# Attention keys split over the two halves of the partitions, so that each score product reads 64 rows

## The reference, cut to what matters

```python
s = jnp.einsum('bqhd,bsd->bqhs', qib, k_idx)                 # indexer, 16 heads of 64
score = jnp.einsum('bqhs,bqh->bqs', jax.nn.relu(s), wb)
_, idx = lax.top_k(score, topk)                              # 256 keys of each query
...
logits = jnp.einsum('bqhd,bqkhd->bhqk', qb, k_sel) * scale   # 8 heads of 64
logits = logits - slopes * dist                              # ALiBi, masked, softmax
```

## Time and profile before

| | before |
|---|---|
| median of 3 runs | 2578.8 us (2577.88 to 2579.78) |
| the profiled execution | 2572.35 us, its span 2570.6 us |
| PE busy | 2484.9 us, 97% |
| DVE, ACT, POOL busy | 1288.5, 846.6, 1064.9 us |
| `projection` | 0 to 465 us |
| `mixers` | 466 us to about 910 us |
| `trunk` | to the end, some 1600 us |

### The profile page before, as it was taken

How to read it: one execution, slowest core, us unless ns; L and a number is a source line. 1 busy time by engine, 2 the same in 40 slices (tenths; PEclk the granted TensorE clock), 3 DMA queues, 4 the chain that set the end, 5 groups by cost and what they waited for, 6 DMA issues and landing times.

```text
span 2570.6 us, 36247 instructions
## 1 busy us (share of the span) xinstructions
PE 2484.9 (97%) x14088; PEld 2136.2 (83%) x14088; DVE 1288.5 (50%) x2467; ACT 846.6 (33%) x1394; POOL 1064.9 (41%) x622
## 2 busy tenths in 40 slices
PE   7999999889999989999999999999999999999997
PEld 7889999668888778898898888888888888888885
DVE  6799999797886433333333433323223332232224
ACT  3684222333443223222222323322333332332222
POOL 1433213454544424444344544444444444454442
PEclk9999999899999999999999999999999999999998
DMA  4101230333333234332232323332333233334331
GB/s 138 34 18 59 79 100 22 107 111 107 103 101 102 87 102 122 97 99 81 84 99 82 92 73 99 93 107 82 96 92 91 81 115 98 89 92 115 109 97 48
DMA packets 274997, 231.39 MB, mean 90 GB/s; under 512 B 10768, under 2 KB 255568, under 8 KB 274832
## 3 DMA queue, kind: packets, MB, share of 16 engines
q1 hardware_dynamic: 266640, 220.59, 28.8%
q10 hardware_dynamic: 8192, 8.52, 0.9%
HBM read 215.81 MB, written 12.71 MB: 89 GB/s over the span
## 4 chain that ended last, share of the span: by engine, by line
PE 59%; DMA 1%; POOL 1%; DVE 0%; ACT 0%; issue 0%; POOLq 0%; SPq 0%; ACTq 0%; DVEq 0%
PE banks L2013 37%; PE banks L2029 20%; PE banks L2065 1%; PE banks L2043 1%; PE banks L2052 1%; DMA cq_raw<-in_w_up 0%; PE banks L1715 0%; DMA last_draw<-in_w_down 0%; POOL dL L1931 0%; POOL wL L1920 0%; POOL wL L1924 0%; DVE y L2233 0%; ACT dH L2115 0%; DVE n_bn L1624 0%; ACT L2124 0%
## 5 line engine op out<-in xcount | busy, mean ns | idle before, releaser
L1924 POOL TENSOR_TENSOR wL<-cq_raw,wH 128x2048 fp32r<-128x2048 f32 x87 | 405.8, 4665 | 529.9 <-ACT wH L2109 529.9
L2013 PE MATMUL banks<-hL,wH 128*128 128x512 f32 (+1 forms) x1760 | 618.3, 351 | 5.0 <-ACT hid L2124 4.8
L2013 PE MATMUL banks<-hH,wL 128*128 128x512 f32 (+1 forms) x1760 | 617.3, 351 | 0.0
L2013 PE MATMUL banks<-hH,wH 128*128 128x512 f32 (+1 forms) x1760 | 615.4, 350 | 0.0
L2213 DVE TENSOR_TENSOR hid<-hid,banks 128x512 f32<-128x512 f32 (+1 forms) x110 | 64.4, 585 | 739.1 <-PE banks L2013 632.2
L2013 PEld LDWEIGHTS banks<-hL,wH 128*128 128x128 f32 x1760 | 330.6, 188 | 54.2 <-ACT hid L2124 5.9
L2013 PEld LDWEIGHTS banks<-hH,wL 128*128 128x128 f32 x1760 | 330.5, 188 | 46.4
L2013 PEld LDWEIGHTS banks<-hH,wH 128*128 128x128 f32 x1760 | 331.1, 188 | 44.9
L1931 POOL TENSOR_TENSOR dL<-last_draw,dH 128x1024 fp32r<-128x1024 f32 x88 | 220.9, 2510 | 332.0 <-ACT dH L2115 331.9
L2233 DVE TENSOR_TENSOR y<-y,banks 128x512 f32<-128x512 f32 (+1 forms) x340 | 233.1, 686 | 203.2 <-PE banks L2029 202.2
L2029 PE MATMUL banks<-dH,hidL 128*128 128x512 f32 (+1 forms) x748 | 296.4, 396 | 2.3 <-issue 2.3
(11 more groups left out here) (257 smaller groups left out, 4224.9 us busy)
## 6 DMA issues: line engine op xcount, KB each, us to landing
cq_raw<-in_w_gate SPq DMA_DIRECT2D x88, 512.0 KB, 4.7
cq_raw<-in_w_up SPq DMA_DIRECT2D x88, 512.0 KB, 5.9
last_draw<-in_w_down SPq DMA_DIRECT2D x88, 512.0 KB, 3.4
w_out_part<-in_w_out SPq DMA_DIRECT2D x60, 512.0 KB, 4.0
va<-in_w_in SPq DMA_DIRECT2D x10, 1024.0 KB, 5.4
va<-in_x SPq DMA_DIRECT2D x8, 512.0 KB, 4.3
vg_scratch<-y ACTq DMA_DIRECT2D x32, 128.0 KB, 1.7
y<-in_x SPq DMA_DIRECT2D x8, 512.0 KB, 7.4
```

Of the source, the lines that this page charges most:

```text
L1924: nc.gpsimd.tensor_tensor(wL[:, ff % 2, :, :, :].rearrange("p g k f -> p (g k f)"), raw[:, :, :, :].rearrange("p g k f -> p (g k f)"), wH[ ...
L2013: last = nc.tensor.matmul(banks[:, GU + (2 * q + g) % 3, 0:n], wt[:, ff % 2, g, k, :], h[:, k, a:a + n], start=(k == 0 and part == 0), sto ...
```

## The change

Keys 0 to 511 of every head now lie in partitions 0 to 63, keys 512 to 1039 in partitions 64 to 127 (`kaT` becomes [128, 8 heads, 528]). The queries of a head are written to both halves, and no zeros are needed. A score product reads the 64 partitions in which its keys lie. Keys come out of PSUM in two copies of 64 partitions, one for each head of the feature tile, and the key chunks are 512, 264 and 264 columns. The scratch for the top-8 values moves into a tile that is free by then.

```diff
+KEY_SPLIT = 512
+def key_rows(a):
+    return (slice(0, HD), 0) if a < KEY_SPLIT else (slice(HD, P), KEY_SPLIT)
...
-                kaT = sb(mixer, "kaT", [P, 4, L])
+                kaT = sb(mixer, "kaT", [P, A_HEADS, L - KEY_SPLIT])
...
-    top8 = sb(c, "top8", [P, NT, 8])
+    top8 = squares[:, 0:NT * 8].rearrange("p (m e) -> p m e", m=NT)
...
-            slab_units += [(j, fm, dest, ft, a, n) for ft in range(SW // P) for a, n in CHUNKS3]
+            slab_units += [(j, fm, dest, ft, a, n) for ft in range(SW // P)
+                           for a, n in (((0, KEY_SPLIT), (KEY_SPLIT, 264), (KEY_SPLIT + 264, 264)) if dest == "ka" else CHUNKS3)]
...
             if dest == "ka":
-                nc.scalar.activation(kaT[:, half * SW // P + idx, a:a + n], banks[:, bank, 0:n], ACT.Copy)\
-                  .then_inc(slab_out, 1)
+                to, base = key_rows(a)
+                for par in range(2):
+                    last = nc.scalar.activation(kaT[to, 2 * (half * SW // P + idx) + par, a - base:a - base + n],
+                                                banks[HD * par:HD * (par + 1), bank, 0:n], ACT.Copy)
+                last.then_inc(slab_out, 1)
...
-            return nc.tensor.matmul(logits[0:n, at:at + kn], qaT[:, m % 2, h, 0:n], kaT[:, h // 2, a:a + kn],
+            r, base = key_rows(a)
+            return nc.tensor.matmul(logits[0:n, at:at + kn], qaT[r, m % 2, h, 0:n], kaT[r, h, a - base:a - base + kn],
                                     start=True, stop=True)
...
             if what == "qa":
-                if m == 0:
-                    act.wait_ge(dve_pads, 2)
-                for par in range(2):
-                    r = slice(HD * par, HD * (par + 1))
-                    to = qaT[r, m % 2, :, 0:n].rearrange("p (f two) t -> p two f t", two=2)[:, par]
-                    ins_ = nc.scalar.activation(to, four(src)[r, :, 0:n], ACT.Copy)
+                for half in range(2):
+                    for par in range(2):
+                        to = qaT[HD * half:HD * (half + 1), m % 2, :, 0:n].rearrange("p (f two) t -> p two f t", two=2)[:, par]
+                        ins_ = nc.scalar.activation(to, four(src)[HD * par:HD * (par + 1), :, 0:n], ACT.Copy)
...
         nc.vector.memset(key[:, 0, :], 0.0).then_inc(dve_pads, 1)
-        nc.vector.memset(qaT[:], 0.0).then_inc(dve_pads, 1)
```

More of the change, by code:

```diff
@@ L1510, in scores_of @@
             else:
-                dve.wait_ge(dve_pads, 3)
+                dve.wait_ge(dve_pads, 2)
             if h == 0:
```

## The result

| | before | after |
|---|---|---|
| median, us | 2575.68 | 2582.57 |
| lowest to highest, 20 runs each | 2569.08 to 2581.05 | 2574.24 to 2590.36 |
| ratio of after to before | | 1.0025 [1.0016, 1.0034] |
| the profiled execution, its span | 2572.35, 2570.6 | 2581.62, 2579.9 |
| mean granted clock of TensorE in the profiled execution | 0.990 | 0.986 |

The change costs 6.9 us, 0.25%. The forecast was -1.3 us and "no change"; the time lies in the range, on the other side of the kernel before. The two profiled executions differ by more, 9.3 us: 3.0 up to the end of `projection`, 4.1 in `mixers` and 2.1 in `trunk`, which the change doesn't touch.

The account below looks back on a forecast made before the run. VectorE bounds tile 1, TensorE tiles 5 to 7; tiles 2 to 4 are mixed. Cost 22.8, less 18.1 gain, 8.0 hidden and 0.8 in tile 8, plus 1.0 and 0.2 for copies: -1.3 us, 2577 us, range 2570 to 2585.

Parts of the forecast that it names:

- The clock: Rival: one more 13.6 us stretch at 1.2 GHz in tiles 2 to 4 costs 6.8 us, giving 2584 us; chance 0.14.
- excursions: TensorE going from 128 to 64 rows and back in a mixer step: 0.38 us each, 56 new ones, 21.3 us.
- what is hidden: Added TensorE time in the mixers that falls into later waits for VectorE and costs nothing: 8.0 us.
- the pairs' gain: Mixer tiles 4 to 8: a step's narrower score product runs beside the wider one, saving 18.1 us.
- 18.1 less 0.8: Saving from paired scores in tiles 4 to 8, less 0.8 us because tile 8 gets nearer to VectorE's own pace.
- The sum of the costs: Mixers: 22.8 us of added TensorE time, less 8.0 us hidden in waits.
- The second product waits for both halves of the first: Rival: only one half of the wide score product has company, gain 12.3 us, not 18.1; 2583 us; chance 0.12.
- Cover of 1.34: Tile 3: TensorE's 1.3 us wait for the output projection's add, with a 1.6 us wait, catches later steps' added time.
- The rival of the fuller cover: Rival: tiles 1 to 4 and 8 show none of the excursions' cost, -8.9 us, 2570 us; chance 0.20.
- ScalarE's copies: Score units before the mixers: longer key copies, 5.5 us more ScalarE work, cost +1.0 us, between nothing and 5.5.
- The queries' copies: Mixers at h = 4: two copies become four of 585 ns once a tile, +0.2 us, bounds 0 and 9.4.

Follow-up runs that it names:

- the filler: One unread 512-column product (two in tiles 1 and 2) in TensorE's h = 1 wait, tiles 1 to 6; kernel before 2570.12 us, kernel after 2571.31.
- the filled kernels: The kernel before and the kernel after, each with the filler in tiles 1 to 6: 2570.12 and 2571.31 us.
- rows64: Kernel before with scores that read the head's own 64 partitions, keys not split, nothing paired: 2592.31 us, ratio 1.0059.
- rows64_fill: Kernel before with unpaired 64-row scores, plus the filler in tiles 1 to 6: 2584.60 us, ratio 1.0040.
- fill_before: Kernel before with the filler in tiles 1 to 6, nothing else: 2570.12 us, ratio 0.9981.
- copies: Kernel before with key chunks of 512, 264, 264 and two copies of each key unit, old layout and scores: 2580.67 us, ratio 1.0023.
- the two halves: Kernel before with the key chunks of 512, 264, 264 alone, 2577.93 us; kernel before with two copies of each key unit alone, 2575.74 us.
- low128: Kernel after with tiles 0 to 3 back at 128-row scores, zeros in the upper half of the queries: 2594.79 us, ratio 1.0079.

## Why the prediction was wrong

**The step that failed** is the sum's silence on the clock. "The clock" stood among the rivals with 0.14, on the ground that more idle time in tiles 1 to 3 might give one more low stretch, 2584 us. The time came out near that rival's (2582.6), but the sum held no term for the clock, and 0.14 was low. I had seen two such stretches in the tiles, one of them right behind the wait at `gram` h = 1, and the same wait stands in tiles 1 to 6. What that ground left out is that it comes again in tiles 4 to 6, where TensorE is the bound right behind it, and that there a stretch costs its full half (6.6 us for 13.7 in tile 5). That the time fits the rival's price is partly luck, since the rival looked for its stretch in tiles 2 to 4. Over the runs mean clock fell by 0.0038: at 1.9 us per 0.001 that is 7.2 us, the whole loss. Runs with the same mean clock (0.986, 0.987, 0.988: 59 of the kernel before, 8 after) show no loss: after is 0.2, 1.9 and 2.7 us faster there. Shown besides: the stretch in tile 5 of the profile after, none in tiles 4 to 6 once the wait is filled, 11.3 us back from the filler and some 1 us left between the filled kernels. My first account of the runs, that the pairs alone do it by making the wait longer, has fallen: `rows64` has the stretch without pairs and with a wait of 0.80 us, hardly more than before. Open: by what the clock falls in one tile and holds in the next, and so what in the change makes it fall more often; 64-row scores are what the profiles point to.

**The sum itself came out near, by errors that cancel.** Tile lengths, from the first `gram` row of one tile to that of the next (tile 8 to the last output quarter), each taken from kernels in which the tile had no low stretch, in us:

| tile | before | 64 rows, no pairs | after | measured | forecast |
|---|---|---|---|---|---|
| 3 | 48.99 | 48.15 | 47.79 | -1.2 | +1.2 |
| 4 | 51.83 | 52.67 | 52.85 | +1.0 | +1.3 |
| 5 | 52.91 | 54.80 | 53.35 | +0.4 | +0.5 |
| 6 | 57.03 | 58.74 | 56.23 | -0.8 | -1.0 |
| 7 | 60.32 | 62.65 | 57.46 | -2.9 | -2.7 |
| 8 | 108.61 | 111.1 | 106.64 | -2.0 | -3.8 |

(111.1 is 112.78 less 1.7 for a short low stretch in it.) Tile 0 was +0.9 against +0.5, tile 1 nothing against +0.5, tile 2 +1.2 against +1.1. The forecast's column is its own terms by tile: 2.7 for seven excursions (3.7 in tile 8), less what is hidden, less the pairs' gain. Measured that makes -3.4 for the mixers against -2.5. The second column takes it apart. What the excursions cost, less what is hidden, is its difference from the first: from tile 3 on -0.8, +0.8, +1.9, +1.7, +2.3 and +2.5, and +0.9 in tile 2 (`rows64_fill` less `fill_before`), 9.3 us in all. The forecast had 13.8 for these tiles. The pairs' gain, the third column less the second, is 13.4 us in tiles 4 to 8, where 18.1 less 0.8 were forecast. So a cost that was some 4.5 us too high stood against a gain that was 4 us too high.

With +3.0 in `projection` in place of +1.0, the stages at full clock add up to -0.4 us, where I had -1.3; by the fit the kernel after comes out 1.2 to 2.0 us below the one before (2572.6 against 2573.8 and 2574.6). Either way the program alone is hardly changed, as forecast.

**An excursion.** 0.38 us was near but high: tile 7, which hides none, lost 2.33 us for seven, 0.33 each; tile 6, of which I had said the same, lost 1.7, 0.24 each. The sum of the costs (22.8 - 8.0 = 14.8) against 14.5 us between the filled kernels looks better than it is, since 0.0023 of mean clock, some 4 us, is in the latter.

**The pairs.** 0.67 us a step in tile 7: measured 62.65 - 57.46 = 5.2 over eight steps, 0.65. Tiles 5 and 6 gave 1.5 and 2.5 in place of 1.9 and 3.7. In tile 8 the pairs gave 4.5 where 6.9 - 0.8 were counted. VectorE's pass over the banks is late next by more than I took off, which is most of the difference: the waits of the whole tile, to be held against the 4.5 of the earlier trace rows:

```profile
PE banks L1197 <- DVE nmax L1459: 5.8, 8, 1.5
```

**"The second product waits for both halves of the first"** has fallen: the rows of two at 812.48 show the second product's first half beside the first's. Taken row by row, the trace contradicts what the Trainium skill says in "TensorE: Matmul & The Clock Gate", Part 3, that matmuls start and end strictly in program order: the second half of the wide product stands behind both first halves.

**What hides the cost** was undersized: tile 4 kept 0.8 us where I had left 1.6, and in tile 3 seven excursions made the tile shorter. Before, late in the tile (h = 5 to 7), in the kernel with the filler:

```profile
612.68 0.66 PE L1155 MATMUL banks<-ident,on 128*128 128x128 f32 x4 [1.34 <-DVE y L1539]
615.01 0.94 PE L1184 MATMUL banks<-kaT,qaT 128*128 128x400 f32 x2 [0.73 <-DVE nmax L1453]
```

The two waits, 2.07 us, are gone after (the step is 3.33 us in place of 5.40). Cover of 1.34 was counted, the wait behind it was not. Why more goes than the delay of some 0.9 us ahead of it, I leave open. The rival of the fuller cover was right for this tile alone.

**ScalarE's copies** were forecast at +1.0 between bounds 0 and 5.5, and this term was mis-sized as well: the scores take 3.0 us longer at full clock (150.97 against 148.01), and the stage ended 3.0 us later in the kernel after, whose `projection` has as much low clock as before (two stretches of 3.4 us for one of 6.8). `copies` cost 4.8 as timed, 1.2 to 2.0 by the fit. What of it is ScalarE's 6.0 us more, what TensorE's long key units beside short score units, is not settled: the two halves cost 0 and 0 alone and 4.8 together. The queries' copies (+0.2) can't be told apart except in tile 0: the tile is 0.9 us longer after but not in `rows64`, which has its 64-row products too, nor in `low128`, which has two copies there, not four.

## What to carry to other kernels

Where a change shortens TensorE's work in front of a wait for another engine, look at what that wait does to the granted clock, not only at its length: it stands in the windows' clock column, and a stretch at 1.2 GHz costs half its length wherever TensorE is the bound. Before giving such a rival a chance, count the places where the same wait comes again with TensorE as the bound behind it. To tell a change's own price from the clock's, give both kernels the same filler at the waits and compare those, read the mean granted clock of every run, and compare runs of the same clock. And a total that comes out near says little of its terms: here a cost and a gain were both 4 us too high.

## What the hardware showed that I had not expected

A kernel's own runs differ by their clock: 1.9 us for each 0.001 of mean clock, over all kernels. A product that nobody reads makes this kernel faster: eight fillers of 1.13 us or so, 6.1 us before, 11.3 after. And fp32 products in different halves of the rows run side by side, each with its first half and then its second: 512 and 400 columns of one step took 1.06 us from start to the next group, way in and all, where 912 columns in 128 rows took 1.53.
